# GpSimd makes the lo halves of the attention stages' weight panels, VectorE takes all convolution taps, and the mask products move ahead of the 64-row ones

## The chip, the cores and the metric

The kernel runs on one core of one Trainium2 chip. The metric is the device time of one execution in microseconds (us). The engines of the core are TensorE (PE in the rows: matmul; PEld is its weight load), VectorE (DVE), ScalarE (ACT), GpSimd (POOL) and SyncE (SP), which only issues transfers here.

## What is computed

Two transformer blocks in a row on 512 tokens of 1024 features, in float32. The first has a gated depthwise convolution of 31 taps on 512 channels beside stick-breaking attention with 8 heads; the second has 8 heads of softmax attention with a forget gate ("fox") beside 4 heads of differential attention ("diff"). Both end in a SwiGLU network. Cut to what the change touches:

```python
u = u_val * sigmoid(u_gate)
u = causal_depthwise_conv(u, conv_w, conv_b)          # 31 taps, 512 channels
u = silu(layernorm(u, conv_ln_g, conv_ln_b))
# stick-breaking attention, per block of 128 queries
z = q @ k.T / sqrt(64)                                # masked: key < query
log_keep = where(causal, log_sigmoid(-z), 0)
a = where(causal, exp(log_sigmoid(z) + log_after), 0);  out = a @ v
merged = sigmoid(g_conv) * y_conv + sigmoid(g_att) * y_att
# second block
fox:  sc = q @ k.T / sqrt(64) + (c[t] - c[s]), masked, softmax, @ v
diff: a = softmax(q1 @ k1.T / sqrt(64) - slope * dist) - lam * softmax(q2 @ k2.T ...);  out = a @ v
```

## The kernel before

The activations are kept transposed, as 8 tiles of 128 features by 512 tokens. Every weight is streamed from memory in panels of 128 by 1024 (8 tiles of 128 by 128), 217 of them, through a ring of three buffers `raw`. Each panel is split into two fp32r halves: ScalarE copies it, rounded, into `w_hi` (line 363), and VectorE subtracts it from the panel to make `w_lo` (line 705). A product of two split numbers is three matmuls: hi by hi, hi by lo and lo by hi (lines 1156 to 1158, called `mul`); a tile of 128 outputs takes 24 of them, 512 columns each.

Each engine has its own program, written by hand, and runs it in that order; semaphores join them. SyncE issues the next panel into a `raw` buffer when `raw_used` says that VectorE has made the half from it (or used it up as one of the modulation panels "ada", line 699, which lie between the later panels). `feed(name, i)` in VectorE's program makes the halves up to two panels ahead of panel i. TensorE's `halves_ready` waits for the same count.

The stages that the change touches, in the order in which they run:

- *q/k of block 1* (`qk1`, 8 tiles). VectorE: `feed`, the lo half of the tile's output (`qk_lo`, line 765), four taps (line 757).
- *v of block 1* (`v1`, 4 panels). VectorE: `feed` and three taps each, `softplus(0)` after the second, then the four `v_lo` (line 772). TensorE's `scores(1)`, which comes after the first gate tile, waits for the third of them because it writes the same PSUM banks.
- *Gates and heads*. TensorE runs, for head n, the suffix sums (line 1277), the weighted v of head n-1, gate tile n+1 and `scores(n+2)`. VectorE: softplus, `feed`, `a_lo`, `head_lo`, four taps. After the heads come gate tiles 9 to 15, with six taps each; behind gate tile 12 TensorE waits for all taps and sums `conv` over the channels (line 1331).
- A tap is one multiply-add of 128 by 512 on VectorE. VectorE has channel tiles 0 to 2, 93 taps. GpSimd has channel tile 3, 31 taps, each as a multiplication into `tap_buf` (line 328) and an addition (line 331).
- *q/k, v, fox and diff heads of block 2.* `softmax_scores` makes a map of 512 queries by up to 512 keys in four pieces. Ahead of the first q/k tile VectorE makes `sel`, `pos` and `slope` (lines 950 to 957), the operands of the row terms, from what GpSimd has laid out after the first block's last panel.

The score products have 64 rows (the head dimension), in either the upper or the lower half of the array. Each piece ends in a mask product of 128 rows in bf16 (lines 1265 and 1435), which adds -1e30 where a key is not allowed:

```python
mul(ps[:, bank, at:at + w], (qk_hi[rows, 4 + n // 2, keys], ...), (qk_hi[rows, n // 2, queries], ...), at == 0, False)
ins = nc.tensor.matmul(ps[:, bank, at:at + P], ident_b[:], mask_kq[:], start=False, stop=True)
```

Of the kernel before, what the change touches and what calls it, by code (L numbers as in the profile page):

```python
# [56 lines left out]
def build(nc, t):
# [4 lines left out]
    with ctx:  # L62
# [223 lines left out]
        def _(pool):  # L286
# [32 lines left out]
            pool.wait_ge(u_ready, CT)  # L319
            for j in range(TAPS):  # L320
                src, weight = u_pad[:, POOL_TILE, j:j + SEQ], col("conv_w", POOL_TILE * TAPS + j)
                if j == 0:
                    nc.gpsimd.tensor_scalar(conv[:, POOL_TILE, :], src, weight, col("conv_b", POOL_TILE), ALU.mult,
                                            ALU.add).then_inc(pool_tap, 1)
                else:
                    if j >= 3:
                        pool.wait_ge(pool_tap, j - 1)
                    nc.gpsimd.tensor_scalar(tap_buf[j % 2][:], src, weight, None, ALU.mult).then_inc(tap_prod, 1)  # L328
                    pool.wait_ge(tap_prod, j)
                    pool.wait_ge(pool_tap, j)  # L330
                    nc.gpsimd.tensor_tensor(conv[:, POOL_TILE, :], conv[:, POOL_TILE, :], tap_buf[j % 2][:], ALU.add)\
                        .then_inc(pool_tap, 1)

            pool.wait_ge(panel_used, FIRST["ffn_out1"] + 22)
# [348 lines left out]
        def _(dve):  # L683
# [219 lines left out]
            dve.wait_ge(raw_used, AT[FIRST["ffn_in1"]])  # L903
# [45 lines left out]
            dve.wait_ge(consts2, 7)  # L949
            nc.vector.tensor_copy(sel[:], sel_f[:]).then_inc(sel_ready, 1)  # L950
            nc.vector.tensor_copy(pos_f[:], pos_i[:]).then_inc(sel_ready, 1)
            dve.wait_ge(sel_ready, 2)
            nc.vector.tensor_copy(pos[:], pos_f[:]).then_inc(sel_ready, 1)
            dve.wait_ge(sel_ready, 3)
            nc.vector.tensor_copy(pos[HD:2 * HD, :], pos_f[0:HD, :]).then_inc(sel_ready, 1)
            for h in range(DH):
                nc.vector.tensor_scalar(slope[:, h, :], ones_d[:], D * 2.0 ** (-8.0 * (h + 1) / DH), None,
                                        ALU.mult).then_inc(sel_ready, 1)
# [676 lines left out]
```

## Time and profile before

| | |
|---|---|
| three timed runs, median (lowest to highest) | 1512.92 us (1512.38 to 1516.34) |
| the profiled execution | 1512.19 us |
| its span | 1510.4 us |
| TensorE matmul busy | 1448.9 us (96%) |
| VectorE busy | 790.4 us (52%) |
| ScalarE busy | 534.2 us (35%) |
| GpSimd busy | 138.2 us (9%) |
| TensorE's granted clock, mean | 0.978 |

Busy times are of one profiled execution. Matmuls overlap, so what counts for TensorE is the time from one start to the next (the pitch), which the rows of a timeline show, and not the duration of one. A row in square brackets ends with the idle time ahead of an instruction and what ended it.

### The profile page before, as it was taken

What the parts mean: (1) busy time and instruction counts of PE and PEld (TensorE: products, weight loads), DVE (VectorE), ACT (ScalarE), POOL (GpSimd) and SP (SyncE); (2) the same over time, 40 slices, a digit from 0 to 9 for tenths busy, and PEclk for the clock granted to TensorE, in tenths of its full rate; (3) what the DMA queues carried; (4) which work ended last, traced back from release to release, by engine and by line L of the source; (5) the groups of instructions that cost most, each with busy time, mean ns of one, the idle gap of its engine ahead of it and who ended that gap; (6) DMA issues with size and microseconds to landing.
All of it is one profiled execution on the core that took longest, in us unless ns stands there. A gap on an engine that the chain in (4) does not pass through costs nothing.

```text
span 1510.4 us, 15824 instructions
## 1 busy us (share of the span) xinstructions
PE 1448.9 (96%) x6432; PEld 1157.8 (77%) x6432; DVE 790.4 (52%) x1052; ACT 534.2 (35%) x792; POOL 138.2 (9%) x104
## 2 busy tenths in 40 slices
PE   8998999989999999999988999999779999999996
PEld 6886888767678888888865888787558888888885
DVE  5799878577674333332237435547755333333332
ACT  4332665343443222222224334343434222232221
POOL 2399900000000000000010000000000000000000
PEclk9999999999999999999999999899899999999998
DMA  9322113446444333323221221101012333332321
GB/s 367 127 84 80 32 43 96 158 131 241 142 131 133 98 98 98 98 84 112 84 84 42 98 84 57 42 29 42 15 56 84 98 98 98 98 98 91 96 86 63
DMA packets 41113, 147.03 MB, mean 97 GB/s; under 512 B 4561, under 2 KB 4817, under 8 KB 40913
## 3 DMA queue, kind: packets, MB, share of 16 engines
q1 hardware_dynamic: 40896, 143.93, 29.8%
q10 hardware_dynamic: 144, 2.10, 0.4%
q8 instruction: 51, 0.84, 0.2%
q14 instruction: 22, 0.17, 0.0%
HBM read 143.91 MB, written 2.10 MB: 97 GB/s over the span
## 4 chain that ended last, share of the span: by engine, by line
PE 82%; DVE 13%; ACT 3%; issue 1%; DMA 0%; DVEq 0%; SPq 0%; ACTq 0%
PE ps L1156 26%; PE ps L1158 25%; PE ps L1157 25%; DVE conv L757 3%; DVE w_lo L705 2%; PE ps L1277 2%; PE ps L1449 1%; DVE t_buf L737 1%; DVE t_buf L723 1%; PE ps L1195 1%; DVE x L732 1%; PE ps L1433 1%; PE ps L1435 1%; DVE qk_lo L765 0%; PE ps L1190 0%
## 5 line engine op out<-in xcount | busy, mean ns | idle before, releaser
L1156 PE MATMUL ps<-h_hi,w_hi 128*128 128x512 f32 x1160 | 457.7, 395 | 6.4 <-DVE w_lo L705 4.3
L1158 PE MATMUL ps<-h_hi,w_lo 128*128 128x512 f32 x1160 | 454.0, 391 | 0.0
L1157 PE MATMUL ps<-h_lo,w_hi 128*128 128x512 f32 x1160 | 454.0, 391 | 0.0
L705 DVE TENSOR_TENSOR w_lo<-raw,w_hi 128x1024 fp32r<-128x1024 f32 x217 | 268.5, 1239 | 283.3 <-ACT w_hi L363 282.8
L363 ACT ACTIVATE w_hi<-raw 128x1024 fp32r<-128x1024 f32 x217 | 228.0, 1053 | 140.4 <-PE ps L1158 117.2
L1156 PEld LDWEIGHTS ps<-h_hi,w_hi 128*128 128x128 f32 x1160 | 219.7, 189 | 55.8 <-DVE w_lo L705 5.6
L1158 PEld LDWEIGHTS ps<-h_hi,w_lo 128*128 128x128 f32 x1160 | 219.2, 189 | 46.3
L1157 PEld LDWEIGHTS ps<-h_lo,w_hi 128*128 128x128 f32 x1160 | 219.6, 189 | 45.2 <-issue 0.5
L1158 PE MATMUL ps<-act_hi,w_lo 128*128 128x512 f32 x352 | 140.4, 399 | 0.0
L1157 PE MATMUL ps<-act_lo,w_hi 128*128 128x512 f32 x352 | 138.7, 394 | 0.0
L1156 PE MATMUL ps<-act_hi,w_hi 128*128 128x512 f32 x352 | 138.0, 392 | 0.0
L536 ACT ACTIVATE act_hi<-sq 128x512 fp32r<-128x512 f32 x44 | 27.8, 632 | 192.3 <-DVE sq L921 192.3
L921 DVE TENSOR_TENSOR sq<-ps,t_buf 128x512 f32<-128x512 f32 x44 | 30.4, 690 | 105.4 <-PE ps L1158 105.4
L757 DVE SCALAR_TENSOR_TENSOR conv<-u_pad,cols,conv 128x512 f32<-128x512 f32 x90 | 83.1, 980 | 0.1
L1157 PEld LDWEIGHTS ps<-act_lo,w_hi 128*128 128x128 f32 x352 | 66.1, 188 | 17.1
L1156 PEld LDWEIGHTS ps<-act_hi,w_hi 128*128 128x128 f32 x352 | 66.1, 188 | 15.9
L1158 PEld LDWEIGHTS ps<-act_hi,w_lo 128*128 128x128 f32 x352 | 66.1, 188 | 15.2
L328 POOL TENSOR_SCALAR tap_buf<-u_pad,cols 128x512 f32<-128x512 f32 x30 | 70.4, 2346 | 0.0
L542 ACT ACTIVATE t_buf<-ps 128x512 f32<-128x512 f32 x44 | 26.3, 597 | 122.9 <-PE ps L1158 122.8
L372 ACT ACTIVATE sq<-x 128x512 f32<-128x512 f32 x40 | 25.2, 631 | 100.2 <-DVE x L1145 67.0
L747 DVE TENSOR_TENSOR acc<-acc,sq 128x512 f32<-128x512 f32 x32 | 22.1, 690 | 65.5 <-ACT sq L518 59.8
L335 POOL MEMSET sel_f<- 128x1024 f32 x1 | 1.0, 951 | 597.4 <-PE ps L1158 597.4
(238 smaller groups left out, 1714.4 us busy)
## 6 DMA issues: line engine op xcount, KB each, us to landing
raw<-in_ffn_in SPq DMA_DIRECT2D x88, 512.0 KB, 3.5
raw<-in_ffn_out SPq DMA_DIRECT2D x44, 512.0 KB, 3.5
raw<-in_ada SPq DMA_DIRECT2D x32, 512.0 KB, 4.5
raw<-in_qk SPq DMA_DIRECT2D x25, 512.0 KB, 3.5
ada<-in_ada SPq DMA_DIRECT2D x16, 512.0 KB, 9.3
raw<-in_gates SPq DMA_DIRECT2D x16, 512.0 KB, 3.5
raw<-in_v SPq DMA_DIRECT2D x12, 512.0 KB, 3.5
raw<-in_glu SPq DMA_DIRECT2D x8, 512.0 KB, 8.4
```

What stands on the lines that cost most here:

```text
L328: nc.gpsimd.tensor_scalar(tap_buf[j % 2][:], src, weight, None, ALU.mult).then_inc(tap_prod, 1)
L363: nc.scalar.activation(w_hi[p % RING][:], raw[AT[p] % RAW][:], ACT.Copy).then_inc(hi_ready, 1)
L372: nc.scalar.activation(buf, src, ACT.Square).then_inc(sq_ready, 1)
L536: nc.scalar.activation(act_hi[:, i, :], sq[i % 2][:], ACT.Copy).then_inc(act_hi_of[name], 1)
L542: nc.scalar.activation(t_buf[i % 2][:], ps[:, 2 * (i % 4), :], ACT.Silu).then_inc(silu_of[name], 1)
L705: nc.vector.tensor_tensor(w_lo[p % RING][:], raw[q % RAW][:], w_hi[p % RING][:].bitcast(f32), ALU.subtract).then_inc(raw_used, 1)
L757: ins = nc.vector.scalar_tensor_tensor(out=conv[:, c, :], in0=src, scalar=col("conv_w", c * TAPS + j), in1=conv[:, c, :], op0=ALU.mult, op ...
L921: nc.vector.tensor_tensor(sq[i % 2][:], ps[:, 2 * (i % 4) + 1, :], t_buf[i % 2][:], ALU.mult)\
L1156: nc.tensor.matmul(out, w[0], v[0], start=start, stop=False, **kw)
L1157: nc.tensor.matmul(out, w[0], v[1], start=False, stop=False, **kw)
L1158: return nc.tensor.matmul(out, w[1], v[0], start=False, stop=stop, **kw)
L1277: ins = nc.tensor.matmul(out, tri[:] if later == kb else negones[:], half[:, KEY_AT[later]:KEY_AT[later] + w], start=False, stop=True, **free)
```

## The change

Four edits.

1. GpSimd makes the `w_lo` of seven groups of panels (`POOL_PANELS`, 48 panels: 28 in the first block, 20 in the second), in its own program, each as soon as its `w_hi` is there. VectorE's `feed` leaves them out. SyncE and TensorE wait on the counter of the engine that has the panel (`taken`).
2. VectorE has all four channel tiles of the convolution, 124 taps: six in place of four behind each `qk1` tile, four in place of three behind each `v1` panel; behind the gates the numbers are as before.
3. In each scores block the four mask products come first, and the 64-row products follow without one between them. In the softmax blocks the waits for the map before stand ahead of the masks.
4. `sel`, `pos` and `slope` are made behind q/k tile 6 of the second block, and GpSimd lays out their sources after the last `h_lo` of that block's first normalisation.

```diff
+POOL_PANELS = ("qk1", "v1", "gates", "v2", "v3", "qk3", "wout_a")
+TAKEN_AT, _n_dve, _n_pool = [], 0, 0
...
+        def taken(q):
+            return raw_used_pool if ITEMS[q][0] in POOL_PANELS else raw_used, TAKEN_AT[q]
...
-        POOL_TILE = CT - 1
-        TAP_ORDER = [(c, j) for j in range(TAPS) for c in range(POOL_TILE)]
+        TAP_ORDER = [(c, j) for j in range(TAPS) for c in range(CT)]
...
-                    sp.wait_ge(raw_used, q - RAW + 1)
+                    sp.wait_ge(*taken(q - RAW))
...
+            def lo_halves(*names):
+                for q, (name, i) in enumerate(ITEMS):
+                    if name in names:
+                        n = FIRST[name] + i
+                        pool.wait_ge(hi_ready, n + 1)
+                        nc.gpsimd.tensor_tensor(w_lo[n % RING][:], raw[q % RAW][:], w_hi[n % RING][:].bitcast(f32),
+                                                ALU.subtract).then_inc(raw_used_pool, 1)
+
+            lo_halves("qk1", "v1", "gates")
+
+            pool.wait_ge(h_ready, 3 * KT)
...
+            lo_halves("v2", "v3", "qk3", "wout_a")
...
-                    else:
+                    elif what not in POOL_PANELS:
...
                 qk_lo_tile("qk1", i, QK1_BANK[i], QK[i], i % 2, qk_hi, qk_lo, i + 1)
-                taps(4)
+                taps(6)
...
                 feed("v1", b)
-                taps(3)
+                taps(4)
...
+            def row_terms():
+                dve.wait_ge(consts2, 7)
+                nc.vector.tensor_copy(sel[:], sel_f[:]).then_inc(sel_ready, 1)
...
+                if i == 6:
+                    row_terms()
...
                 for kb in range(NB):
                     c, at = KEY_BANK[kb]
+                    nc.tensor.matmul(ps[:, 3 * (n % 2) + c, at:at + P], ident_b[:], mask_kq[:], start=at == 0,
+                                     stop=False, **free)
+                for kb in range(NB):
+                    c, at = KEY_BANK[kb]
...
-                    ins = nc.tensor.matmul(ps[:, bank, at:at + P], ident_b[:], mask_kq[:], start=False, stop=True, **free)
...
                     if n and qb != 1:
                         pe.wait_ge(s_exp, NB * (n - 1) + max(qb + 1, 2))
+                    nc.tensor.matmul(ps[:, bank, at + P * qb:at + P * (qb + 1)], ident_b[:], mask_qk[:],
+                                     start=at == 0, stop=False, **free)
+                for qb in range(NB):
```

VectorE in the q/k stage of the first block, two tiles, before:

```order
L765 SCALAR_TENSOR_TENSOR qk_lo<-ps,qk_scale,qk_hi 128x512
L757 SCALAR_TENSOR_TENSOR conv<-u_pad,cols,conv 128x512 x4
L705 TENSOR_TENSOR w_lo_67<-raw_61,w_hi_64 128x1024
L765 SCALAR_TENSOR_TENSOR qk_lo<-ps,qk_scale,qk_hi 128x512
L757 SCALAR_TENSOR_TENSOR conv<-u_pad,cols,conv 128x512 x4
```

and now:

```order
L765 SCALAR_TENSOR_TENSOR conv<-u_pad,cols,conv 128x512 x6
L773 SCALAR_TENSOR_TENSOR qk_lo<-ps,qk_scale,qk_hi 128x512
L765 SCALAR_TENSOR_TENSOR conv<-u_pad,cols,conv 128x512 x6
L773 SCALAR_TENSOR_TENSOR qk_lo<-ps,qk_scale,qk_hi 128x512
L765 SCALAR_TENSOR_TENSOR conv<-u_pad,cols,conv 128x512 x6
```

The `w_lo` went to GpSimd, and two more taps stand behind each tile.

VectorE behind the last head (`qk_lo` by line 838), gate tiles 9 to 12; `raw` by itself is an ada product, and the last row takes the mean off after TensorE's sum over `conv`. Before:

```order
L838 TENSOR_TENSOR qk_lo<-ps,qk_hi 64x512
L699 SCALAR_TENSOR_TENSOR raw_61,mod<-raw_61,c_all 128x1024
L705 TENSOR_TENSOR w_lo_68<-raw_62,w_hi_65 128x1024
L757 SCALAR_TENSOR_TENSOR conv<-u_pad,cols,conv 128x512 x6
L699 SCALAR_TENSOR_TENSOR raw_63,mod<-raw_63,c_all 128x1024
L705 TENSOR_TENSOR w_lo_69<-raw_61,w_hi_66 128x1024
L757 SCALAR_TENSOR_TENSOR conv<-u_pad,cols,conv 128x512 x6
L699 SCALAR_TENSOR_TENSOR raw_62,mod<-raw_62,c_all 128x1024
L705 TENSOR_TENSOR w_lo_67<-raw_63,w_hi_64 128x1024
L757 SCALAR_TENSOR_TENSOR conv<-u_pad,cols,conv 128x512
L699 SCALAR_TENSOR_TENSOR raw_61,mod<-raw_61,c_all 128x1024
L705 TENSOR_TENSOR w_lo_68<-raw_62,w_hi_65 128x1024
```

and now:

```order
L846 TENSOR_TENSOR qk_lo<-ps,qk_hi 64x512
L707 SCALAR_TENSOR_TENSOR raw_61,mod<-raw_61,c_all 128x1024
L765 SCALAR_TENSOR_TENSOR conv<-u_pad,cols,conv 128x512 x6
L707 SCALAR_TENSOR_TENSOR raw_63,mod<-raw_63,c_all 128x1024
L765 SCALAR_TENSOR_TENSOR conv<-u_pad,cols,conv 128x512 x6
L707 SCALAR_TENSOR_TENSOR raw_62,mod<-raw_62,c_all 128x1024
L765 SCALAR_TENSOR_TENSOR conv<-u_pad,cols,conv 128x512 x6
L707 SCALAR_TENSOR_TENSOR raw_61,mod<-raw_61,c_all 128x1024
L765 SCALAR_TENSOR_TENSOR conv<-u_pad,cols,conv 128x512 x6
L876 SCALAR_TENSOR_TENSOR conv<-ps,conv 128x512 x4
```

24 taps stand here now, where 13 stood.

TensorE in a fox scores block (the row prints 128 columns of weights as 128 rows; `m_hi` and `m_lo` have 64 rows), before:

```order
L1158 MATMUL ps<-w_hi_65,h_lo 128x512
L1156 MATMUL ps<-m_hi 128x128
L1157 MATMUL ps<-m_lo,m_hi 128x128
L1158 MATMUL ps<-m_hi,m_lo 128x128
L1433 MATMUL ps<-fc_hl,sel 128x128
L1435 MATMUL ps<-mask_qk,ident_b 128x128
L1156 MATMUL ps<-m_hi 128x256
L1157 MATMUL ps<-m_lo,m_hi 128x256
L1158 MATMUL ps<-m_hi,m_lo 128x256
L1433 MATMUL ps<-fc_hl,sel 128x256
L1435 MATMUL ps<-mask_qk,ident_b 128x128
L1156 MATMUL ps<-m_hi 128x384
```

and now:

```order
L1169 MATMUL ps<-w_hi_65,h_lo 128x512
L1440 MATMUL ps<-mask_qk,ident_b 128x128 x4
L1167 MATMUL ps<-m_hi 128x128
L1168 MATMUL ps<-m_lo,m_hi 128x128
L1169 MATMUL ps<-m_hi,m_lo 128x128
L1449 MATMUL ps<-fc_hl,sel 128x128
L1167 MATMUL ps<-m_hi 128x256
L1168 MATMUL ps<-m_lo,m_hi 128x256
L1169 MATMUL ps<-m_hi,m_lo 128x256
L1449 MATMUL ps<-fc_hl,sel 128x256
L1167 MATMUL ps<-m_hi 128x384
```

The four masks stand ahead of all the rest.

## Rows read from the trace of the kernel before

**Rows 1.** The page, part 4: the chain that ended last, by engine.
```profile
PE 82%; DVE 13%; ACT 3%; issue 1%; DMA 0%; DVEq 0%; SPq 0%; ACTq 0%
```
**Rows 2.** Timeline of TensorE: start us, us, engine, line, operation [idle ahead <- what ended it].
```profile
146.46 0.49 PE L1156 MATMUL ps<-qk_hi 64*128 64x512 f32 x1 [3.92 <-DVE v_lo L772]
...
278.18 3.60 PE L1331 MATMUL ps<-conv,ones_d 128*128 128x512 f32 x8
```
**Rows 3.** TensorE's waits: us in total, times, longest.
```profile
PE ps L1494 <- ACT sq L633: 6.7, 3, 3.6
PE ps L1156 <- DVE w_lo L705: 6.7, 4, 2.6
```
**Rows 4.** Timeline of VectorE, q/k stage, columns as in Rows 2.
```profile
72.62 0.75 DVE L765 SCALAR_TENSOR_TENSOR qk_lo<-ps,qk_scale,qk_hi 128x512 fp32r<-128x512 f32 x1 [2.90 <-ACT qk_hi L394]
...
78.81 4.59 DVE L757 SCALAR_TENSOR_TENSOR conv<-u_pad,cols,conv 128x512 f32<-128x512 f32 x4
...
85.12 4.20 DVE L757 SCALAR_TENSOR_TENSOR conv<-u_pad,cols,conv 128x512 f32<-128x512 f32 x4
...
115.45 4.57 DVE L757 SCALAR_TENSOR_TENSOR conv<-u_pad,cols,conv 128x512 f32<-128x512 f32 x4
```
**Rows 5.** Timeline of VectorE, gate tiles 9 to 12.
```profile
257.86 1.23 DVE L699 SCALAR_TENSOR_TENSOR raw<-raw,c_all 128x1024 f32<-128x1024 f32 x1
...
261.14 4.06 DVE L757 SCALAR_TENSOR_TENSOR conv<-u_pad,cols,conv 128x512 f32<-128x512 f32 x6
```
**Rows 6.** Timeline of GpSimd, additions of the taps.
```profile
74.37 1.34 POOL L331 TENSOR_TENSOR conv<-conv,tap_buf 128x512 f32<-128x512 f32 x1
...
134.05 1.53 POOL L331 TENSOR_TENSOR conv<-conv,tap_buf 128x512 f32<-128x512 f32 x1
...
182.37 1.29 POOL L331 TENSOR_TENSOR conv<-conv,tap_buf 128x512 f32<-128x512 f32 x1
```
**Rows 7.** Timeline of VectorE, a `w_lo` and the four `v_lo` of the v stage.
```profile
134.35 2.31 DVE L705 TENSOR_TENSOR w_lo<-raw,w_hi 128x1024 fp32r<-128x1024 f32 x1
...
144.53 2.47 DVE L772 TENSOR_TENSOR v_lo<-ps,v_hi 128x512 fp32r<-128x512 f32 x4
```
**Rows 8.** Stretches: length; busy us (instructions) of PE, PEld, DVE, ACT, POOL; clock; DMA; GB/s.
```profile
146.40:154.00 7.60, 7.54 (x26) 5.72 (x27) 6.62 (x7) 2.52 (x4) 7.43 (x5) 0.55 0.21 71
860.00:1046.00 186.00, 186.00 (x889) 147.54 (x888) 96.22 (x187) 74.25 (x176) 0.00 (x0) 0.94 0.17 52
```
**Rows 9.** Timeline of TensorE, a stick-breaking scores block.
```profile
216.07 0.39 PE L1158 MATMUL ps<-h_hi,w_lo 128*128 128x512 f32 x1
216.39 0.50 PE L1156 MATMUL ps<-qk_hi 64*128 64x512 f32 x1
216.72 0.39 PE L1157 MATMUL ps<-qk_lo,qk_hi 64*128 64x512 f32 x1
216.96 0.39 PE L1158 MATMUL ps<-qk_hi,qk_lo 64*128 64x512 f32 x1
217.28 0.23 PE L1265 MATMUL ps<-mask_kq,ident_b 128*128 128x128 bf16 x1
217.44 0.44 PE L1156 MATMUL ps<-qk_hi 64*128 64x384 f32 x1
...
219.55 0.47 PE L1277 MATMUL ps<-sb_hi,tri 128*128 128x512 f32 x1
```
**Rows 10.** Timeline of TensorE, a fox scores block: its first product and the next block's.
```profile
917.35 0.32 PE L1156 MATMUL ps<-m_hi 64*128 64x128 f32 x1
...
921.15 0.47 PE L1156 MATMUL ps<-h_hi,w_hi 128*128 128x512 f32 x1
```
**Rows 11.** Timeline of VectorE, the row terms and the stage they move into.
```profile
817.12 0.69 DVE L950 CAST sel<-sel_f 128x1024 fp32r<-128x1024 f32 x1
...
819.65 1.22 DVE L705 TENSOR_TENSOR w_lo<-raw,w_hi 128x1024 fp32r<-128x1024 f32 x1
...
854.66 0.75 DVE L765 SCALAR_TENSOR_TENSOR m_lo<-ps,qk_scale,m_hi 128x512 fp32r<-128x512 f32 x1 [3.27 <-ACT m_hi L394]
```

More of the change, by code:

```diff
@@ L53 @@
 N_PANELS = len(AT)
+POOL_PANELS = ("qk1", "v1", "gates", "v2", "v3", "qk3", "wout_a")
+TAKEN_AT, _n_dve, _n_pool = [], 0, 0
+for _name, _i in ITEMS:
+    if _name in POOL_PANELS:
+        _n_pool += 1
+        TAKEN_AT.append(_n_pool)
+    else:
+        _n_dve += 1
+        TAKEN_AT.append(_n_dve)
 assert ITEMS[-1] == ("ffn_out2", 21) and sum(n == "ada" for n, _ in ITEMS) == 48 - FIRST_ADA
@@ L130, in build @@
         tri_f = place("tri_f", [P, P], f32, at=A0 + 93 * K)
-        tap_buf = [place(f"tap_buf{i}", [P, SEQ], f32, at=A0 + 94 * K + 2 * K * i) for i in range(2)]
         gate_a = place("gate_a", [P, KT, SEQ], f32, at=A0 + 48 * K)
@@ L166, in build @@
                                                          sem("ada_dots_done"))
+        raw_used_pool = sem("raw_used_pool")
         cols_in, c_in, x_again, lam_in, out_done = (sem("cols_in"), sem("c_in"), sem("x_again"),
@@ L317, in _ @@
                     .then_inc(mod_ready, 1)
[L319 to L324, printed above, removed]
-                else:
[L326 to L334, printed above, removed]
+            def lo_halves(*names):
[7 more added lines that the diff above has]
+            pool.wait_ge(h_ready, 3 * KT)
             nc.gpsimd.memset(sel_f[:], 0.0).then_inc(consts2, 1)
@@ L701, in feed @@
                                                        accum_out=mod[:, j:j + 1]).then_inc(raw_used, 1)
-                    else:
+                    elif what not in POOL_PANELS:
                         p = FIRST[what] + j
@@ L902, in _ @@
                 add_square(KT + m)
[L903 removed]
+            dve.wait_ge(raw_used, TAKEN_AT[AT[FIRST["ffn_in1"]] - 1])
             link(nc.vector.tensor_tensor(mod[:, 16:40], mod[:, 16:40], col("ada_b", 16, 24), ALU.add))
@@ L947, in _ @@
             link(nc.vector.tensor_scalar(lam_s[:, 6:7], col("diff_norm_g_2"), 1.0 - LAM_INIT, None, ALU.mult))
[L949 to L958, printed above, removed]
+            def row_terms():
+                dve.wait_ge(consts2, 7)
+                nc.vector.tensor_copy(sel[:], sel_f[:]).then_inc(sel_ready, 1)
+                nc.vector.tensor_copy(pos_f[:], pos_i[:]).then_inc(sel_ready, 1)
+                dve.wait_ge(sel_ready, 2)
+                nc.vector.tensor_copy(pos[:], pos_f[:]).then_inc(sel_ready, 1)
+                dve.wait_ge(sel_ready, 3)
+                nc.vector.tensor_copy(pos[HD:2 * HD, :], pos_f[0:HD, :]).then_inc(sel_ready, 1)
+                for h in range(DH):
+                    nc.vector.tensor_scalar(slope[:, h, :], ones_d[:], D * 2.0 ** (-8.0 * (h + 1) / DH), None,
+                                            ALU.mult).then_inc(sel_ready, 1)
             def flog_sums():
@@ L1164, in halves_ready @@
             def halves_ready(name, i):
-                pe.wait_ge(raw_used, AT[FIRST[name] + i] + 1)
+                pe.wait_ge(*taken(AT[FIRST[name] + i]))
             def tile(name, i, bank, moving):
@@ L1258, in scores @@
                     c, at = KEY_BANK[kb]
+                    nc.tensor.matmul(ps[:, 3 * (n % 2) + c, at:at + P], ident_b[:], mask_kq[:], start=at == 0,
+                                     stop=False, **free)
+                for kb in range(NB):
+                    c, at = KEY_BANK[kb]
                     w = SEQ - P * kb
-                    bank = 3 * (n % 2) + c
                     keys, queries = slice(P * kb, P * (kb + 1)), slice(P * kb, SEQ)
-                    mul(ps[:, bank, at:at + w],
-                        (qk_hi[rows, 4 + n // 2, keys], qk_lo[rows, 4 + n // 2, keys]),
-                        (qk_hi[rows, n // 2, queries], qk_lo[rows, n // 2, queries]), at == 0, False, **free)
-                    ins = nc.tensor.matmul(ps[:, bank, at:at + P], ident_b[:], mask_kq[:], start=False, stop=True, **free)
+                    ins = mul(ps[:, 3 * (n % 2) + c, at:at + w],
+                              (qk_hi[rows, 4 + n // 2, keys], qk_lo[rows, 4 + n // 2, keys]),
+                              (qk_hi[rows, n // 2, queries], qk_lo[rows, n // 2, queries]), False, True, **free)
                 ins.then_inc(z_done, 1)
@@ L1431, in softmax_scores @@
                     mul(out, (m_hi[rows, q_tile, queries], m_lo[rows, q_tile, queries]),
-                        (m_hi[rows, k_tile, 0:w], m_lo[rows, k_tile, 0:w]), at == 0, False, **free)
+                        (m_hi[rows, k_tile, 0:w], m_lo[rows, k_tile, 0:w]), False, False, **free)
                     nc.tensor.matmul(out, row_term[0][rows, row_term[1], :], row_term[2][rows, 0:w],
-                                     start=False, stop=False, **free)
-                    ins = nc.tensor.matmul(ps[:, bank, at + P * qb:at + w], ident_b[:], mask_qk[:], start=False,
-                                           stop=True, **free)
-                    ins.then_inc(s_done, 1)
+                                     start=False, stop=True, **free).then_inc(s_done, 1)
             def transpose_map(n, buf):
```

5 lines of the change are left out of this document (2 added, 3 removed).

## The prediction

> **What bounds the kernel now.** I read the page's chain first, then TensorE's waits, then the timelines of the stretches that the diff touches. TensorE holds 82% of the chain and VectorE 13% [rows 1]. So a gain has to come out of TensorE's own products, or out of one of its few waits. Among these, two belong to code that the change touches: 3.9 us for `v_lo` ahead of `scores(1)` [rows 2], and 6.7 us in four pieces for `w_lo` [rows 3], of which the longest, 2.6 us, stands at the start of the second block's q/k tiles. GpSimd and VectorE matter only where they end such a wait, or where a longer queue makes a new one.
>
> **How the two engines share time.** In the q/k stage VectorE has no pause: per tile one `w_lo`, one `qk_lo` and four taps (4.20 to 4.59 us in all) [rows 4]. A `w_lo` beside an idle GpSimd takes 1.22 us [rows 11]; 0.09 of it lies under the next start, which leaves 1.13. The same taps take 0.66 us each once GpSimd is idle (six in 4.06, less the 0.08 that ends overlap) [rows 5], so four should take 2.73. The mean of 4.20 and 4.59 is 4.39: 1.66 us are lost per tile. GpSimd's additions start at 74.37, at 134.05 and 14 times between them, one in 4.0 us [rows 6]; the taps of tiles 1 and 7 start at 78.81 and 115.45, which is 6.1 us a tile [rows 4], so 1.52 additions fall into it, and VectorE loses 1.09 us to each. One such addition with VectorE idle takes 1.29 us [rows 6], so the loss is 0.85 of its length. One row shows how: a `w_lo` that began 0.3 us after the addition of 134.05 took 2.31 us and not 1.21, and its last 1.1 us lie behind the addition's end at 135.6 [rows 6, 7]. Two-input operations of the two engines exclude each other.
>
> The new GpSimd `w_lo` has 1024 columns where the addition has 512. No row shows it. It can't be shorter than 1.29 us and should not be longer than twice that, 2.58, since the fixed part is paid once. I take 2.5 us, and 0.85 of it, 2.1 us, as VectorE's loss to each.
>
> **The change, part by part.**
>
> (a) *Taps and panels up to `scores(1)`.* VectorE goes from 72.6, its first `qk_lo` [rows 4], to 144.5, its first `v_lo` [rows 7], with almost no pause: 71.9 us. From it fall 11 `w_lo` at 1.13 (12.4 us) and the loss to 18 additions at 1.09 (19.6). To it come 20 taps at 0.66 (13.2; 64 now against 44) and the loss to 12 GpSimd `w_lo` at 2.1 (25.2; one panel in each TensorE tile of 24 products, some 5.5 us). The sum is +6.4 us, and TensorE has waited for this `v_lo` since 142.5 and starts at 146.46 [rows 2], so this is **+6.4 us** on the path. If a GpSimd `w_lo` cost VectorE only half its length (1.25), it would be -3.8; if it cost 2.58, +12.2. I keep the middle, since the factor 0.85 is from the same stage and the same kind of operation. TensorE itself does not wait for these panels: the half is made right behind the ScalarE half, some 9 us before the tile that reads it.
>
> (b) *The gates after the last head.* VectorE begins with an ada product at 257.86, when TensorE lets go of head 7. It had 13 taps left, it now has 24 (124 less 48, 16, 4 and 32). 24 taps at 0.66 are 15.9 us, four ada products at 1.15 are 4.6, two or three GpSimd `w_lo` (of gate panels 12 to 14) cost 2.1 each, 5.3 us in the mean. VectorE ends at 283.7; TensorE came for the taps at 278.18 and found them ready [rows 2, 5]. That is a **new wait of 5.5 us** in which nothing else can run, since the product over `conv` is next in TensorE's queue. Bounds: 3.6 with two panels at 1.5, 8.6 with three at 2.58. What follows (mean, variance, merge) is chained to TensorE and moves with it.
>
> (c) *The clock behind (b).* Behind the wait of 3.9 us at 146.46 the granted clock averages 0.55 over the 7.6 us to 154, so 3.4 us of full speed are lost [rows 8]. I add **2.0 us** for the same behind the new wait (nothing at best, 3.4 at worst). The drop behind (a) is paid already.
>
> (d) *Mask products.* Before, each scores block went from 64-row to 128-row products and back four times. In the stick-breaking block the pitch at 512 columns is 0.23 us; from the last tile's product to the first 64-row one it is 0.32, from the last 64-row one of this width to the mask 0.32, and from the mask, which has 128 columns of bf16, to the next 0.16 [rows 9]. The block takes 3.16 us (216.39 to 219.55). Its 12 products at their pitches (three each at 0.23, 0.18, 0.115 and 0.112) are 1.9; with one pause in and one out, 2.1. Four masks in a row cost 0.04 to 0.11 each (the pitch of 128 columns of f32 is 0.11). Result 2.3 to 2.5, so 0.65 to 0.9 us less. The fox block takes 3.80 us [rows 10]; 16 products are 2.55, pauses 0.17, masks 0.16 to 0.44: 2.9 to 3.15, the same saving. I take 0.75. Of 24 blocks the first lies ahead of the wait of (a) and gains nothing, and three of the eight diff blocks stand in the stretch from 1046 to 1106, where TensorE waits for the normalisation of the heads (6.7 us in three pieces for `sq`) [rows 3]. 20 times 0.75 is **-15.0 us** (20 times 0.6 at least). The masks now wait for the last exponential of the map before, ahead of any product; there is a whole tile or a P times V product between them, and no row of TensorE between 860 and 1040 has a wait, so I cost that at nothing.
>
> (e) *The row terms.* `sel`, `pos` and `slope` took VectorE from 817.12 to 819.65 [rows 11], ahead of the `w_lo` for which TensorE waited 2.6 us [rows 3]. They move behind tile 6 of the stage, where VectorE idles 3.27 us ahead of the next `m_lo` [rows 11]. The wait goes and nothing is late in its place: **-2.6 us**. The GpSimd memset and selects now run beside it, outside the path.
>
> (f) *The second attention.* There VectorE idles a third of the time and TensorE never waits for it; panels move to GpSimd at no price either way.
>
> (g) *The clock in the attention stages.* From 860 to 1046 no wait is shown, yet the granted clock averages 0.94, which is 11 us of full speed lost [rows 8]. These are stretches at 1.2 GHz that begin during or behind scores blocks. Blocks with fewer pauses should cause fewer of them. What it brings no row tells: from nothing to all 11 us. I take **-3.0**, about a quarter.
>
> Sum: 6.4 + 5.5 + 2.0 - 15.0 - 2.6 - 3.0 = -6.7 us. The profiled execution took 1512.2, of which 1510.4 is the span, so the changed one would take 1505.5. The three timed runs have a median of 1512.9, 0.7 above the profiled one; I put the forecast between the two bases: **1506 us**.
>
> **A rule against (a).** The row says that a `w_lo` was held for the rest of a GpSimd addition [rows 7]. The Trainium skill (SBUF — State Buffer, "SBUF: two separate sides") has it as an exclusive lock that one holds for its whole instruction while the other fully blocks; by that rule each GpSimd `w_lo` would cost VectorE its whole 2.5 us and not 0.85 of it, and (a) and (b) would be 4.8 and 1.0 us dearer, giving 1512. The trace agrees on the single row and falls short of it over the stage (1.09 lost of 1.29). The skill (GPSIMD Engine Reference, section 3.1) measures 4497 ns for 2048 columns of such an operation; an estimate of 2.4 us for 1024 follows from it, which no run here shows.
>
> **The rivals.**
> 1. *GpSimd holds VectorE back more than it relieves it (slower).* Place: taps ahead of `v_lo` and of the mean. If each new `w_lo` costs VectorE L, (a) is 12L - 18.8 and (b) 2.5L + 0.2. The gains (d), (e), (g) less (c) are 18.6, so it decides from 14.5L = 37.2, L = 2.57 us: the full doubled addition. At L = 3.0, where the f32r output makes it longer than twice 512 columns, the result is 6.3 us over the time of before: 1519. For it: the full block of rows 7. Against: 0.85 over the stage. Chance 0.13.
> 2. *The clock gives nothing back, and half of the pauses stay.* The pause may belong to the change of type at the mask and not to the number of rows; then four masks cost 0.16 each and a stick-breaking block takes 2.74, which saves 0.42. Against it stands the pitch of 0.32 from an f32 to an f32 product [rows 9]. Then (d) is -8.4. With (g) at nothing too the time is 1515.6; with the first alone 1512.6, with the second alone 1509. Chance 0.25.
> 3. *VectorE is freer than I think.* If GpSimd yields and L is 1.3, (a) is -3.2 and (b) 3.5: 1494. Chance 0.10.
> 4. *The forecast.* 1501 to 1511, chance 0.50. The last 0.02 is for what I don't see.
>
> **How the numbers follow.** A difference under 0.3%, 4.5 us, can't be told from no change here; the bounds are 1508.4 and 1517.5. The forecast gives 0.40 to faster and 0.10 to same; rival 2 gives 0.03 and 0.22; rival 3 gives 0.10 to faster; rival 1 gives 0.05 to same and 0.08 to slower; the last 0.02 goes to slower. So faster 0.53, same 0.37, slower 0.10. The range from 1494 to 1518 takes in rivals 2 and 3 and the milder half of rival 1.
>
> **What would show it.** (a): the wait ahead of `scores(1)` at 9 us, a GpSimd `w_lo` near 2.5 us with VectorE idle, taps of 0.66 outside them. (b): a wait of 4 to 7 us at the product over `conv`, named for the last tap. (d): scores blocks of 2.4 and 3.0 us. (e): no wait at the third q/k tile of the second block. (g): a clock above 0.95 from 860 to 1046. It would be wrong if GpSimd needed over 3 us a panel, or if the masks in a row were as dear as the switches that they replace.

## The result, and the profile after

| | before | after |
|---|---|---|
| median of four timed runs (lowest to highest) | 1513.55 us (1512.38 to 1516.34) | 1496.37 us (1495.26 to 1498.69) |
| span of the profiled execution | 1510.4 us | 1494.4 us |
| TensorE busy | 1448.9 us | 1421.9 us |
| VectorE / GpSimd busy | 790.4 / 138.2 us | 770.2 / 147.6 us |

The change is faster by 1.1%: ratio 0.9886, 95% interval 0.9867 to 0.9904, which is 17.2 us, where the prediction had 7. The direction was right, and the size was more than twice the forecast.

TensorE's waits in the changed kernel (us in total, times, longest) against [rows 3]: `sq` went from 6.7 to 8.2, `w_lo` from 6.7 to 4.8. The first of the two long waits below is that of [rows 2], which was 3.9; the other did not exist.

```profile
PE ps L1343 <- DVE conv L765: 8.7, 1, 8.7
PE ps L1270 <- DVE v_lo L780: 8.3, 1, 8.3
PE ps L1507 <- ACT sq L641: 8.2, 3, 4.3
PE ps L1167 <- DVE w_lo L713: 4.8, 4, 2.3
```

So the changed kernel waits some 13 us more in these rows, and is 16 us shorter in its span. The gain must lie in TensorE's own stretches. These are the stretches of the kernel before, cut at the same events in both programs (length; busy us of PE, PEld, DVE, ACT, POOL; clock; DMA; GB/s). The cuts are the first scores block, `scores(1)`, `scores(2)`, the last stick-breaking block, the sum over `conv`, the first fox block, the first diff block, and the end of the last diff block (the last row is what follows it):

```profile
109.87:146.46 36.59, 32.56 (x138) 25.64 (x137) 36.52 (x35) 14.05 (x17) 35.76 (x20) 0.95 0.29 86
146.46:160.87 14.41, 14.41 (x61) 11.37 (x61) 11.84 (x12) 7.50 (x10) 14.08 (x9) 0.76 0.11 38
160.87:229.87 69.00, 69.00 (x361) 56.18 (x360) 54.55 (x61) 42.85 (x60) 25.66 (x13) 0.98 0.13 39
229.87:278.18 48.31, 47.53 (x237) 39.80 (x237) 40.27 (x55) 22.65 (x30) 0.00 (x0) 1.00 0.41 129
859.27:1003.73 144.46, 144.46 (x688) 115.86 (x687) 70.58 (x131) 56.27 (x123) 0.00 (x0) 0.95 0.18 56
1003.73:1068.45 64.72, 63.46 (x314) 47.60 (x313) 41.80 (x89) 28.47 (x77) 0.00 (x0) 0.95 0.10 33
1068.45:1510.40 441.95, 412.25 (x1783) 334.28 (x1783) 178.42 (x220) 127.12 (x171) 0.00 (x0) 0.97 0.27 84
```

and the same stretches of the changed kernel:

```profile
108.50:146.73 38.23, 29.91 (x138) 24.55 (x137) 38.16 (x46) 13.95 (x17) 13.14 (x5) 0.95 0.25 83
146.73:161.93 15.20, 15.20 (x60) 13.20 (x60) 9.90 (x12) 7.49 (x10) 1.84 (x1) 0.67 0.00 1
161.93:225.20 63.27, 63.27 (x361) 54.76 (x361) 49.83 (x56) 42.75 (x60) 17.28 (x6) 1.00 0.14 42
225.20:281.42 56.22, 46.88 (x238) 39.80 (x237) 53.32 (x58) 26.08 (x33) 17.56 (x7) 0.95 0.39 121
861.49:993.15 131.66, 131.66 (x688) 110.41 (x687) 51.75 (x115) 56.49 (x123) 38.06 (x16) 1.00 0.21 64
993.15:1049.30 56.15, 53.97 (x313) 43.80 (x313) 38.47 (x87) 28.05 (x77) 5.00 (x3) 1.00 0.13 39
1049.30:1494.40 445.10, 414.69 (x1783) 335.34 (x1782) 179.44 (x220) 127.09 (x171) 0.00 (x0) 0.96 0.26 83
```

Read the first number after each pair of times. Up to the sum over `conv` the changed kernel gives away 1.6 + 0.8 + 7.9 us and takes back 5.7 in the gates with heads; the fox maps bring 12.8 and the diff maps 8.6. The stretch behind them is 3.1 us longer: TensorE waits 0.7 us more for `sq` there, and the clock is 0.96 and not 0.97. What is not in these rows: the start (108.8 and 107.5 us to the first scores block) and the middle from 278.18 or 281.42 to the first fox block (581.1 and 580.1). The differences sum up to 16.0 us. Read the clock too, the third number from the end (1.00 is 2.4 GHz throughout, and each part of a stretch at the lower level, 1.2 GHz, takes from it): the fox and diff stretches were granted 0.95 before, and 1.00 after.

### The profile page after: what moved, and what is told of

It reads as the page before. It is cut to its first block, busy times and chain, and to the rows that moved or that the text cites. A ratio compares the mean times of both kernels' runs of the same rounds, so it can differ in the third digit from the quotient of the medians.

```text
span 1494.4 us, 15763 instructions
## 1 busy us (share of the span) xinstructions
PE 1421.9 (95%) x6432; PEld 1149.4 (77%) x6432; DVE 770.2 (52%) x1035; ACT 533.7 (36%) x792; POOL 147.6 (10%) x91
## 4 chain that ended last, share of the span: by engine, by line
PE 79%; DVE 15%; ACT 4%; issue 1%; DMA 0%; DVEq 0%; SPq 0%; ACTq 0%
PE ps L1167 25%; PE ps L1169 25%; PE ps L1168 25%; DVE conv L765 6%; PE ps L1290 1%; DVE w_lo L713 1%; PE ps L1462 1%; DVE t_buf L745 1%; DVE t_buf L731 1%; DVE raw L707 1%; PE ps L1206 1%; PE ps L1449 1%; DVE x L740 1%; PE ps L1507 0%; PE ps L1343 0%
## 5 line engine op out<-in xcount | busy, mean ns | idle before, releaser
L713 DVE TENSOR_TENSOR w_lo<-raw,w_hi 128x1024 fp32r<-128x1024 f32 x169 | 207.2, 1228 | 247.8 <-ACT w_hi L371 247.7
L336 POOL TENSOR_TENSOR w_lo<-raw,w_hi 128x1024 fp32r<-128x1024 f32 x48 | 124.3, 2591 | 291.8 <-ACT w_hi L371 291.8
L765 DVE SCALAR_TENSOR_TENSOR conv<-u_pad,cols,conv 128x512 f32<-128x512 f32 x120 | 120.5, 1068 | 0.1
L1168 PEld LDWEIGHTS ps<-act_lo,w_hi 128*128 128x128 f32 x352 | 66.1, 188 | 17.2
```

Of the source, the lines that this page charges most:

```text
L336: nc.gpsimd.tensor_tensor(w_lo[n % RING][:], raw[q % RAW][:], w_hi[n % RING][:].bitcast(f32), ALU.subtract).then_inc(raw_used_pool, 1)
L713: nc.vector.tensor_tensor(w_lo[p % RING][:], raw[q % RAW][:], w_hi[p % RING][:].bitcast(f32), ALU.subtract).then_inc(raw_used, 1)
L765: ins = nc.vector.scalar_tensor_tensor(out=conv[:, c, :], in0=src, scalar=col("conv_w", c * TAPS + j), in1=conv[:, c, :], op0=ALU.mult, op ...
L1168: nc.tensor.matmul(out, w[0], v[1], start=False, stop=False, **kw)
```

## The experiments

Each ratio is to runs of the kernel before on the same chip. A difference in us is one of medians, and each row is of one profiled execution. All of the first four were made to take the change apart.

**1. The masks alone.** Edit 3 on the kernel before:

```diff
+for kb in range(NB): matmul(ps[.. at:at + P], ident_b, mask_kq, start=at == 0, stop=False)
 for kb in range(NB):
     mul(...)
-    matmul(ps[.. at:at + P], ident_b, mask_kq, start=False, stop=True)
```

> The kernel before with edit 3 alone (mask products ahead). Theory 1: the masks carry the whole gain and the panel split gives some of it back. 22 blocks that stand behind the first wait, 0.76 us each and 0.07 of pause beside them, are 18 us; if the higher granted clock of the second attention belongs to the masks too, 7 us more: 1488 to 1494, with the blocks at 2.4 and 3.06 us, the wait for v_lo at about 5 us, no wait at the sum over conv and a clock of 0.99 or more from the first fox block to the end of the heads. Theory 2: the clock's gain comes with the panel split (fewer VectorE operations beside TensorE) or by chance: then the blocks shrink in the same way, but the clock stays at 0.94 to 0.95 there: 1496 to 1500.

Measured: 1488.18 us, ratio 0.9832 (0.9807 to 0.9857). That is 26 us less than before, and 8 us less than the full change. The stretches from `scores(2)` to the end of the last stick-breaking block (72.17 us at a clock of 0.98 before), of the fox maps and of the diff maps:

```profile
162.51:228.15 65.64, 65.64 (x377) 56.80 (x376) 57.71 (x65) 43.34 (x61) 27.80 (x13) 1.00 0.17 49
855.61:987.27 131.66, 131.66 (x687) 110.37 (x687) 70.40 (x131) 56.27 (x123) 0.00 (x0) 1.00 0.21 61
987.27:1043.41 56.14, 53.96 (x313) 43.75 (x312) 40.62 (x89) 28.03 (x77) 0.00 (x0) 1.00 0.13 38
```

The fox maps take 131.66 us, to the hundredth what the full change takes, with GpSimd idle (0.00). So the higher clock there has nothing to do with the panels: theory 1 stands.

**2. The panels and taps alone.** Edits 1 and 2 on the kernel before, with masks and row terms as before:

```diff
+POOL_PANELS = ("qk1", "v1", "gates", "v2", "v3", "qk3", "wout_a")
-        TAP_ORDER = [(c, j) for j in range(TAPS) for c in range(POOL_TILE)]
+        TAP_ORDER = [(c, j) for j in range(TAPS) for c in range(CT)]
```

> The kernel before with edits 1 and 2 alone (GpSimd makes the lo halves of 48 panels, VectorE all taps), masks and row terms as before. Theory 1: slower. VectorE reaches v_lo 1.5 us later, TensorE waits some 8.8 us at the sum over conv (VectorE needs 29 us from the last head to its last tap, TensorE 20), and 2 to 3 us of clock go behind it: 1522 to 1527. Theory 2: the split gives a part of the gain, through the clock or w_lo waits that go: 1505 to 1513.

Measured: 1527.01 us, ratio 1.0096 (1.0063 to 1.0130), slower by 12.6 us by the medians and 14.5 by the ratio. TensorE's two waits are 8.0 us for `v_lo` and 8.7 us at the sum over `conv`. This half of the change is a loss of its own.

```profile
PE ps L1338 <- DVE conv L765: 8.7, 1, 8.7
PE ps L1164 <- DVE v_lo L780: 8.0, 1, 8.0
```

The fox stretch of this kernel, whose masks lie between the pieces, has the low clock again, 0.93:

```profile
873.51:1021.02 147.51, 147.51 (x688) 117.65 (x687) 52.29 (x115) 57.23 (x123) 38.02 (x16) 0.93 0.19 57
```

**3. Masks and row terms.** Edits 3 and 4 on the kernel before, `row_terms()` behind tile 6 as in the change.

> The kernel before with edits 3 and 4 (masks ahead, row terms later), panels and taps as before. Theory 1: masks_only less the 2.6 us wait for w_lo at the third q/k tile of the second block, 1486 to 1492, and faster than the full change by 4 to 10 us, since neither of its longer waits (8.3 ahead of scores(1), 8.7 at the sum over conv) is there. Theory 2 (the split brings the clock): slower than the full change, 1497 or more.

Measured: 1484.31 us, ratio 0.9805 (0.9779 to 0.9830), 3.9 us less than with the masks alone. The row at the third q/k tile of the second block, without and with the move:

```profile
816.02 0.80 PE L1156 MATMUL ps<-h_hi,w_hi 128*128 128x512 f32 x1 [2.62 <-DVE w_lo L705]
```

```profile
810.34 0.50 PE L1159 MATMUL ps<-h_hi,w_hi 128*128 128x512 f32 x1 [0.58 <-DVE w_lo L705]
```

2.0 of the forecast 2.6 us went; 0.6 of the wait stays, since another `w_lo` is then the last. The rest of the 3.9 is not the move's as far as the rows show: the wait for `v_lo` in the first block was 2.3 us here and 3.9 with the masks alone. The three parts give -26.2, -3.9 and +12.6, in sum -17.5 us, and the whole change -17.2. They add up, but that they meet so closely is luck: the interval of experiment 2 alone reaches from 9.5 to 19.7 us.

**4. VectorE alone.** The changed kernel with no panel for GpSimd, and all taps on VectorE:

```diff
-POOL_PANELS = ("qk1", "v1", "gates", "v2", "v3", "qk3", "wout_a")
+POOL_PANELS = ()
```

> The changed kernel with no panel left to GpSimd: VectorE makes every w_lo and has all 124 taps, GpSimd idles through both attentions. Theory 1: a GpSimd w_lo costs VectorE 1.8 to 2.1 us where its own costs 1.13, and a GpSimd addition 1.15 where its own tap costs 0.66, so VectorE is soonest done alone: 64 to 65 us from its first qk_lo to its first v_lo (73.4 in the changed kernel, 71.9 before), a wait of 0 to 1 us ahead of scores(1), one of 4 to 5 at the sum over conv, 1481 to 1487. Rival: relieving VectorE of panels is what keeps it from ending later; then 12 w_lo at 1.13 come on top, the wait ahead of scores(1) is over 10 us and the time 1500 or more.

Measured: 1481.73 us, ratio 0.9787 (0.9759 to 0.9815), 14.6 us less than the changed kernel. VectorE has 11 more `w_lo` to make up to `v_lo`, and comes to it 9.6 us sooner after its first `qk_lo` (63.8 us, where the changed kernel took 73.4 and the one before 71.9):

```profile
73.68 0.75 DVE L773 SCALAR_TENSOR_TENSOR qk_lo<-ps,qk_scale,qk_hi 128x512 fp32r<-128x512 f32 x1 [3.29 <-ACT qk_hi L402]
...
137.44 2.48 DVE L780 TENSOR_TENSOR v_lo<-ps,v_hi 128x512 fp32r<-128x512 f32 x4
```

TensorE comes to `scores(1)` and does not stop:

```profile
140.37 0.39 PE L1169 MATMUL ps<-h_hi,w_lo 128*128 128x512 f32 x1
140.59 0.40 PE L1270 MATMUL ps<-mask_kq,ident_b 128*128 128x128 bf16 x4
```

The rival (that GpSimd relieves VectorE) had foretold 1500 or more. The wait at the sum over `conv` was forecast at 4 to 5 us and is 5.7.

**5. Two more taps behind each head.** On experiment 4:

```diff
                     head_lo(h - 1, qk_hi, qk_lo, o_hi, o_ready)
-                taps(4)
+                taps(6)
```

> all_vector with six taps in place of four behind each head (8 left for the gates after the last head, where 24 were). VectorE idles 1.5 to 3.4 us a head there, two taps are 1.33 us. If the wait of 5.7 us at the sum over conv is only VectorE's count of taps, it goes, with 2 to 3 us of clock behind it: 1473 to 1477. Rival: the taps delay softplus, a_lo or the next w_lo, and TensorE waits in the heads instead: 1480 or more.

Measured: 1473.99 us, ratio 0.9734 (0.9720 to 0.9749). The wait at the sum over `conv` is gone from the waits, none came in the heads, and 7.7 us went, more than the wait itself: without it the eight products of the sum took 3.60 us and not 5.70, since the clock had not dropped. This kernel beats the one before and the changed one, which it undercuts by 22 us.

**6. Masks behind.** The changed kernel with the four masks of a block together, behind the 64-row products in place of ahead of them.

> The changed kernel with the four masks together behind the 64-row products of a block, not ahead of them. Theory 1 (what costs is each change between 128-row and 64-row products): blocks of 2.4 and 3.06 us as in the changed kernel, time within 3 us of it unless the later release of the first piece makes ScalarE late. Rival (the place ahead of the block hides the masks behind what came before): blocks longer by 0.2 us or more each, 5 us in all.

Measured: 1499.51 us, ratio 0.9908 (0.9890 to 0.9925), 3.1 us more than the changed kernel, though the intervals overlap (the changed kernel's reaches up to 0.9904). A block, counted from its first product, is shorter behind than ahead, 2.26 against 2.39 us and 2.95 against 3.06. Most of that is how a block is cut: the pause on the way to the first 64-row product lies ahead of it here and within it there. The fox stretch, which has both in, is 131.34 us and not 131.66, so the rival's reason is refuted and the place saves 0.04 us a block. What is lost is in the diff maps, 60.84 us against 56.15. There TensorE idles 5.0 us and not 2.2, because VectorE gets a map later and TensorE waits for `prob_d`; the rest, 1.8 us, is a clock of 0.97 against 1.00, which other kernels have there too (experiment 8). The waits from 990 to 1060:

```profile
PE ps L1507 <- ACT sq L641: 5.4, 2, 3.2
PE ps L1462 <- DVE prob_d L1038: 2.7, 2, 1.5
```

In the changed kernel no wait for `prob_d` stands there.

**7. Half a mask.** The kernel before, masks between the pieces, each mask product with the 64 rows of its head, which leaves out half of the mask:

```diff
-ident_b[:], mask_qk[:]
+ident_b[rows, :], mask_qk[rows, :]
```

> The kernel before, with masks between the pieces as there, but each mask product takes only the 64 rows of its head, so half of the mask is left out. Theory 1 (rows): the change of type to bf16 stays, the change of row count goes; fox blocks of 2.9 to 3.1 us, stick-breaking ones of 2.4. Rival (type): blocks stay at 3.16 and 3.80. On the clock: if it follows the changes of row count, it is 0.99 or more over the fox and diff heads as in the changed kernel, if it follows the interleaved bf16 products, 0.94 to 0.95 as before.

Measured: 1492.00 us in a single run. The timeline of TensorE in a stick-breaking block, to be held against [rows 9]:

```profile
212.71 0.50 PE L1156 MATMUL ps<-qk_hi 64*128 64x512 f32 x1
213.05 0.39 PE L1157 MATMUL ps<-qk_lo,qk_hi 64*128 64x512 f32 x1
213.28 0.39 PE L1158 MATMUL ps<-qk_hi,qk_lo 64*128 64x512 f32 x1
213.51 0.23 PE L1265 MATMUL ps<-mask_kq,ident_b 64*128 64x128 bf16 x1
213.55 0.42 PE L1156 MATMUL ps<-qk_hi 64*128 64x384 f32 x1
...
215.20 0.49 PE L1277 MATMUL ps<-sb_hi,tri 128*128 128x512 f32 x1
```

Before, the mask began 0.32 us after the product ahead of it and held the next for 0.16. Now it is 0.23 (the plain pitch at 512 columns) and 0.04. The block takes 2.49 us and not 3.16, a fox block 3.14 and not 3.80, though the type changes as often as before. So 0.67 us a block belong to the change of the row count. The rest is for the type: 0.1 us up to the 2.39 us of the masks put together, and 0.09 for the pause on entry, which still stands ahead of the block here (the product behind a mask is followed after 0.26 us at 384 columns, and after 0.18 in the changed kernel). The clock goes with it, at four bf16 products between the pieces as before:

```profile
854.30:987.47 133.17, 133.17 (x688) 110.24 (x687) 70.38 (x131) 56.28 (x123) 0.00 (x0) 1.00 0.20 62
```

The Trainium skill (TensorEngine Tiling (Array Packing), "Key Properties") says that a change of the tiling mode drains TensorE. The row above and the ones of [rows 9] agree with that, and give the price. Before, a block has three ways out to 128 rows and back, since nothing returns behind its fourth mask, and both kernels have one last way out to the suffix sums. So one round trip costs 0.67 / 3, or 0.22 us; the two pitches around the first mask say the same, 0.48 less 0.27.

**8. Masks between the pieces in the fox maps alone.** The changed kernel with the old order in the fox maps, and the new one in the stick-breaking and diff maps.

> The changed kernel with the masks of the fox maps between the pieces again, those of the diff and stick-breaking maps ahead. If masks between the pieces cause the drops of the granted clock where they stand: fox blocks of 3.8 us and longer, a clock of 0.94 to 0.96 over the eight fox heads and of 0.99 or more over the diff maps up to the last; some 6 us of blocks and 5 to 7 us of clock over the changed kernel, 1507 to 1510. If the clock there is chance, it is 1.00 over the fox heads, or low over the diff maps too: 1501 to 1503.

Measured: 1510.86 us in a single run, 14.5 more than the changed kernel. The fox and the diff stretches of one execution:

```profile
862.34:1006.66 144.32, 144.32 (x687) 115.72 (x686) 52.38 (x115) 57.12 (x123) 37.96 (x16) 0.95 0.18 59
1006.66:1064.24 57.58, 55.39 (x314) 44.56 (x313) 38.63 (x87) 28.07 (x77) 5.03 (x3) 0.97 0.12 38
```

The fox stretch is 12.7 us longer than in the changed kernel. A fox head at full clock takes 12.43 us with the masks between and 11.60 with them ahead (the starts of two neighbouring blocks: 917.35 and 929.78 before, 917.94 and 929.54 after); eight times 0.83 are 6.6. The other 6.1 us are clock. Of that 1.6 lie in three scores blocks (4.07, 4.36 and 4.59 us long, where the other five take 3.80) and the rest outside them, in products of 128 rows. The diff stretch, with its masks ahead, is 1.4 us longer than the changed kernel's, at a clock of 0.97: there the expected 0.99 did not come.

Over the fox stretch the clock was 0.93, 0.95 and 0.95 in the three kernels profiled here whose fox masks of 128 rows lie between the pieces (2, 8 and the one before), and 1.00 in seven (1, 3, 4, 5, 6, 7 and the changed kernel). That is too regular for chance. TensorE had no wait in any of these stretches.

The other two stretches do not sort themselves like that. Over the diff maps the clock was 0.95 before and 0.97 in experiment 2, both with the masks between, and without 128-row masks between the pieces 1.00 in three kernels (1, 4 and the changed one) and 0.97 in five (3, 5, 6, 7 and 8). From `scores(2)` to the last stick-breaking block it was 0.98 before, but 1.00 in experiment 2, whose masks lie between as well. What a few us of clock do there is not shown to belong to the masks.

**9. Panels of the second block on GpSimd.** Experiment 5 with `POOL_PANELS = ("v2", "v3", "qk3", "wout_a")`.

> all_vector_taps6 with the 20 panels v2, v3, qk3 and wout_a left to GpSimd as in the changed kernel. Theory 1: VectorE idles a third of the time there and TensorE waits for no w_lo, so nothing changes in either direction: within 2 us of all_vector_taps6 (1472 to 1476), the fox and diff stretches 131.7 and 56 to 58 us. Rival: GpSimd's share slows VectorE's map work and the last heads come later: 1477 or more; or it takes some of the w_lo waits away: 1471 or less.

Measured: 1471.82 us, ratio 0.9722 (0.9701 to 0.9742), no different from experiment 5. The fox stretch is 131.66 us again. Term (f), at nothing either way, was right, though VectorE idles nearly half of the time there (96.22 of 186.00 us busy, [rows 8]) and not a third.

**10. Masks behind in the stick-breaking and fox maps, ahead in the diff maps.** On experiment 5.

> all_vector_taps6 with the masks behind the 64-row products in the stick-breaking and fox maps and ahead of them in the diff maps. Theory 1 (from masks_last: blocks 0.12 us shorter in all maps, but waits for prob_d in the diff maps): 16 blocks at 0.12 are 1.9 us, no wait comes: 1471 to 1473. Rival: the later release of the first pieces is paid somewhere in the heads: 1474 or more.

Measured: 1472.34 us, ratio 0.9724 (0.9703 to 0.9744), not told apart from 5 or 9. The forecast of 0.12 us a block went by the block's own length; the fox stretch is shorter by 0.4 us in eight blocks, the 0.04 of experiment 6. The time of experiments 5, 9 and 10 is what the runs can tell; any of them is the version to keep, 5 being the plainest.

## Why the prediction was right and wrong

**The terms against the experiments.**

| terms | forecast | measured alone |
|---|---|---|
| (a), (b), (c): taps and panels | +13.9 us | +12.6 us (experiment 2) |
| (d), (g): masks and their clock | -18.0 us | -26.2 us (experiment 1) |
| (e): row terms | -2.6 us | -3.9 us (3 less 1; 2.0 of it in the wait) |
| sum | -6.7 us | -17.5 us |

**The step that failed is (g).** The prediction read the 0.94 of [rows 8], counted 11 us of full speed lost, and for want of a row took a quarter. The three stretches whose clock was low got nearly all of it back. By the clock of the stretches before, 144.46 us at 0.95 lost 7.2 us, the diff maps' 64.72 at 0.95 lost 3.2, and the heads' 69.00 at 0.98 lost 1.4: together 11.8 us. What is left of the three stretches' gains, when each scores block is counted at the 0.83 us of full clock, is 6.2, 2.8 and 1.6, or 10.6 us (the diff stretch with its 0.9 us more of waiting added back). (g) had 3.0. Of the 10.6 only the 6.2 of the fox maps are shown to be the masks', by experiments 7 and 8; the other two stretches vary by as much among kernels with the same masks, and the changed kernel lost some 2 us of clock again behind the diff maps. Experiment 1's total, 26.2 us less 21 to 23 blocks at 0.83, gives 7 to 9 us for the clock, with an interval of 4 us either way. Even the 6.2 us are twice what (g) had. The error was to treat a loss that stood beside the thing to be removed as if it were mostly something else's. What was missing is a row without it, and one was there to be asked for: whether any stretch without such switches had lost its clock while TensorE did not wait.

**(d) was right in its mechanism and a little short in size and count.** The blocks came out at 2.39 and 3.06 us, forecast 2.3 to 2.5 and 2.9 to 3.15. But a head became 0.83 us shorter and not 0.75: the pause on entry, which stood ahead of the block, is inside it now. A block of the changed kernel shows how: four masks in 0.32 us, one pause on entry, none between the pieces, and the pitch of [rows 9] otherwise.

```profile
212.55 0.40 PE L1270 MATMUL ps<-mask_kq,ident_b 128*128 128x128 bf16 x4
212.87 0.50 PE L1167 MATMUL ps<-qk_hi 64*128 64x512 f32 x1
213.21 0.39 PE L1168 MATMUL ps<-qk_lo,qk_hi 64*128 64x512 f32 x1
213.44 0.39 PE L1169 MATMUL ps<-qk_hi,qk_lo 64*128 64x512 f32 x1
213.67 0.34 PE L1167 MATMUL ps<-qk_hi 64*128 64x384 f32 x1
...
214.94 0.49 PE L1290 MATMUL ps<-sb_hi,tri 128*128 128x512 f32 x1
```

The three diff blocks that were left out because TensorE waits for `sq` among them counted too: the diff stretch became 8.6 us shorter, though TensorE idled 0.9 us more in it. The fear of a mask that waits for the exponential of the map before was idle: no wait stands in the fox stretch.

**(a) and (b) were each wrong, and nearly cancelled.** (a) was forecast at +6.4, and scores(1) began 0.3 us later than before. The price of a GpSimd `w_lo` was right where it meets taps for its whole length. Three groups of six taps, beside one `w_lo`, beside none, and, after the last head, beside two:

```profile
93.52 6.18 DVE L765 SCALAR_TENSOR_TENSOR conv<-u_pad,cols,conv 128x512 f32<-128x512 f32 x6
...
108.55 4.05 DVE L765 SCALAR_TENSOR_TENSOR conv<-u_pad,cols,conv 128x512 f32<-128x512 f32 x6
...
253.43 8.34 DVE L765 SCALAR_TENSOR_TENSOR conv<-u_pad,cols,conv 128x512 f32<-128x512 f32 x6
```

6.18 less 4.05 is 2.13, half of 8.34 less 4.05 is 2.14; the forecast was 2.1. Its length, taken as 2.5, is 2.39 us beside an idle VectorE and 2.35 to 3.04 beside a busy one:

```profile
66.80 2.39 POOL L336 TENSOR_TENSOR w_lo<-raw,w_hi 128x1024 fp32r<-128x1024 f32 x1 [3.40 <-ACT w_hi L371]
```

But not all twelve meet taps for their whole length. One, at 134.63, fell on `softplus`, where only the copy `sb_hi` was longer (1.38 us, and 0.83 in experiment 4). VectorE took 73.4 us from `qk_lo` to `v_lo`, 1.5 more than before and not 6.4; as it also began 1.2 us sooner, `v_lo` moved by 0.3.

```profile
71.41 0.75 DVE L773 SCALAR_TENSOR_TENSOR qk_lo<-ps,qk_scale,qk_hi 128x512 fp32r<-128x512 f32 x1 [4.91 <-ACT qk_hi L402]
...
144.79 2.48 DVE L780 TENSOR_TENSOR v_lo<-ps,v_hi 128x512 fp32r<-128x512 f32 x4
```

Experiment 4 tells the two parts of the 4.9 us apart. Its 63.8 us less eleven `w_lo` of its own at 1.13 are 51.4, so the twelve of GpSimd cost VectorE 22.0 us in the changed kernel, 1.8 each: 3.2 us less than forecast. The other 1.7 are what (a) had too much for VectorE without GpSimd, 71.9 - 19.6 + 13.2 = 65.5 against 63.8. The wait of 8.3 us looks like the forecast 9, but for another reason. TensorE came 4.1 us sooner (138.4 against 142.5), and VectorE hardly later. TensorE had begun its first scores block 1.4 us sooner, the block was 0.8 us shorter, and behind its start the clock did not drop (0.76 over 6.1 us before, 1.00 now).

(b) was forecast at 5.5, from "two or three" panels at 2.1. There are four between the last head and the last tap:

```profile
254.46 2.63 POOL L336 TENSOR_TENSOR w_lo<-raw,w_hi 128x1024 fp32r<-128x1024 f32 x1 [5.65 <-ACT w_hi L371]
258.36 2.86 POOL L336 TENSOR_TENSOR w_lo<-raw,w_hi 128x1024 fp32r<-128x1024 f32 x1 [1.27 <-ACT w_hi L371]
267.76 2.52 POOL L336 TENSOR_TENSOR w_lo<-raw,w_hi 128x1024 fp32r<-128x1024 f32 x1 [6.54 <-ACT w_hi L371]
272.67 2.35 POOL L336 TENSOR_TENSOR w_lo<-raw,w_hi 128x1024 fp32r<-128x1024 f32 x1 [2.39 <-ACT w_hi L371]
```

Four at 2.13 are 8.5 and not 5.3, which is the 3.2 us between the forecast wait and the measured one. The bounds beside it, 3.6 and 8.6, were added up wrong as well; the terms of (b) give 3.2 and 7.9, and the 8.66 lies outside them.

```profile
281.42 5.27 PE L1343 MATMUL ps<-conv,ones_d 128*128 128x512 f32 x6 [8.66 <-DVE conv L765]
```

(c) had the right sign: from 281.42 to 288.00 the granted clock was 0.63, which is 2.4 us lost, forecast 2.0.

**The rivals.** Rival 1, slower by the panels, had the mechanism and the place of experiment 2, but a price from L = 2.57 on, and L was 2.13. Rival 2 is refuted in both halves: over the fox maps the clock gave everything back, and by experiment 7 it is mostly the row count that costs, 0.67 of the 0.83 us a head. Rival 3 named the right time, 1494, for a wrong reason: GpSimd did not yield. The rule of the Trainium skill on the shared port (SBUF — State Buffer, "SBUF: two separate sides") would have had VectorE lose the whole of each `w_lo`. It lost 2.13 of 2.4 on taps, close to that, and in experiment 4, with GpSimd idle, nothing. The page grants the lock against VectorE's operations with two SBUF inputs or in a two-port mode; of the two `softplus` operations in question, the one with an input from PSUM (`sb_e`) ran at 1.61 us both times, as the page has it. The copy `sb_hi`, with one input from SBUF, was longer all the same; in which mode it ran no row shows.

## What to carry to other kernels

Small products that change TensorE between 128 and 64 rows are to be put together, ahead of the block when someone waits for its first piece: each round trip costs 0.22 us on the spot, and over the fox maps, with 32 such masks in 144 us, the clock fell to its lower level for some of the time, which cost almost as much again. Where the profile shows lost clock right at a pattern that a change removes and TensorE has no wait there, put the whole loss into the range's favourable end with a real chance. Work moved from VectorE to GpSimd is priced by what it takes from VectorE while both read SBUF, 2.13 us (1.8 in the mean of twelve) against the 1.13 of doing it there, and the first trial is to move nothing at all.
